# One encoder layer on one core: the opening works on 256 tokens first, with part of its statistics on ScalarE and its parameter rows spread by TensorE

## The chip, the cores and the metric

The program runs on one core of one Trainium2 chip. The metric is the device time of one execution in microseconds (us); the kernel before took 1932.78 us, the median of three runs from 1931.15 to 1933.4. Less is better. A core has five engines, each with its own queue worked in order: TensorE (PE; its weight loads are listed as PEld), VectorE (DVE), ScalarE (ACT), GpSimd (POOL) and SyncE (SP, here used to start DMA transfers; ScalarE starts some too). They wait for each other by semaphores.

## The reference

One layer of an encoder over x of 2048 tokens x 1024 features, in float32:

```python
h = layer_norm(x, in_ln_g, in_ln_b)
proj = h @ w_in[l]                       # 1024 -> 1792 features: q, k, v and u
q, k, v, u = jnp.split(proj, [Q_END, K_END, V_END], axis=-1)
... rotary on q and k; windowed attention with sinks; GLU, causal convolution of width 31, LayerNorm, silu on u
mix = jnp.concatenate([attn, conv], axis=-1) @ w_o[l]
h = layer_norm(ALPHA * h + mix, ln1_g[l], ln1_b[l])
ffn = conv_gated_mlp(h, w_up[l], ffn_conv_w[l], ffn_conv_b[l], w_down[l])
h = layer_norm(ALPHA * h + ffn, ln2_g[l], ln2_b[l])
```

The change touches the first two lines only: the first LayerNorm and the start of the projection.

## The kernel before

The phase in question (`phase_project`, tensors named a_...) takes the tokens in NB = 4 blocks of 512, each of RB = 4 rows of 128 tokens; "row (n, r)" is row r of block n. On a row this is done:

- SyncE loads it into `a_xs` (512 KB). VectorE takes two `bn_stats` of 512 columns each (`stats`), and for all four rows of the block together the aggregates, variance plus epsilon (`a_vs`), a root by ScalarE (`block_root`), a reciprocal and three small operations that refine it (`refine_rstd`), and minus mean times that (`a_nmr`).
- The row is normalised and scaled by g, then shifted by b (`scale`, `shift`, each a VectorE pass over 1024 columns). In row 3 of a block ScalarE does the normalising (`norm_last`), VectorE the product with g, GpSimd the sum with b (`shift_last`). g and b stand in `a_gb`, copied to all partitions.
- TensorE transposes the row in eight pieces of 128 x 128 (`transposes`, to `a_acc`). ScalarE rounds the result to a high part (`hi_of`), VectorE makes the low part as the rest (`lo_of`). These are the two halves of `a_hT`. Weights are split into high and low part likewise by ScalarE (`weights_hi`) and GpSimd (`weights_lo`).
- A product is three matmuls of 512 columns (high x high, high x low, low x high). `sweeps(n, first, last)` does products first to last-1 of block n: 24 of them, 8 for each of three lists of 128 output features, each list into a bank of its own (`a_mm`).

What sets the order is code written by hand. Block n-1 is swept while block n is prepared: the four transposes of block n stand between its products, after as many as `AHEAD` says. Product 0 of block n waits until `lo_of` of all four rows of block n is done. When list 1 of block n-1 is done (product 15), ScalarE loads a table and takes the gate's sigmoid (`take_gate`), which stands in its queue between `hi_of(n, 1)` and `hi_of(n, 2)`. After the opening (the four blocks) the other lists of weights follow, 4 x 8 products each, then the convolution, attention, and the feed-forward stage, all led by TensorE.

To keep TensorE at work at the start, it transposes the identity matrix into a bank that nobody reads (`keep_busy`).

## Time and profile before

| | |
|---|---|
| median of 3 runs | 1932.78 us (1931.15 to 1933.4) |
| the profiled execution's own time | 1929.07 us |
| its span (first to last instruction) | 1927.3 us |
| TensorE matmul busy | 1872.7 us, 97% |
| VectorE, ScalarE, GpSimd busy | 1533.2, 942.0, 908.5 us |

The rows of the profile come from the one profiled execution. A row names the line of the kernel, the engine, the operation and the tensors written and read. In the rows, matmuls overlap their neighbours, so a row's duration is longer than the distance to the next start. The granted clock of TensorE is 1.00 at 2.4 GHz and 0.50 at 1.2 GHz.

### The profile page before, as it was taken

The numbers are of one execution on the slowest core, as the hardware profiler recorded it, in microseconds if no ns is written. First come the engines' busy times: TensorE is split into PE (matmuls) and PEld (weight loads), VectorE is DVE, ScalarE is ACT, GpSimd is POOL, SyncE is SP. The second block draws the span as 40 slices with busy tenths as digits, with TensorE's granted clock in tenths as the row PEclk, the third lists the DMA queues.
The fourth block names the chain that finished last, engine by engine and source line by source line (L and its number), as shares of the span: only waits on it lengthen the run. The fifth ranks groups of instructions, "written<-read, shape, count | busy, mean of one in ns | idle before, by whom it ended". The sixth has DMA issues, their size and how long they took to land.

```text
span 1927.3 us, 27509 instructions
## 1 busy us (share of the span) xinstructions
PE 1872.7 (97%) x8632; PEld 1531.4 (79%) x8632; DVE 1533.2 (80%) x1945; ACT 942.0 (49%) x1469; POOL 908.5 (47%) x666
## 2 busy tenths in 40 slices
PE   8999999999999799999999799999999999999998
PEld 7788888777777588888887688888888788888886
DVE  8877993799998788878788888888888745776787
ACT  3455562777776444444445444444444433232453
POOL 2169993266675255444445544443443765530000
PEclk9999999999999899999999899999999999999999
DMA  7411123644553432323232322323234654587654
GB/s 272 174 43 44 44 82 121 204 136 146 176 189 120 148 110 95 117 93 103 103 114 77 131 104 98 118 88 109 93 120 136 197 160 134 166 253 244 186 172 143
DMA packets 200430, 258.41 MB, mean 134 GB/s; under 512 B 12208, under 2 KB 131248, under 8 KB 199856
## 3 DMA queue, kind: packets, MB, share of 16 engines
q1 hardware_dynamic: 188624, 230.37, 36.3%
q10 hardware_dynamic: 11744, 27.27, 3.8%
q8 instruction: 32, 0.52, 0.1%
q14 instruction: 30, 0.25, 0.0%
HBM read 172.98 MB, written 84.61 MB: 134 GB/s over the span
## 4 chain that ended last, share of the span: by engine, by line
PE 57%; issue 18%; DVE 11%; POOL 6%; ACT 5%; DMA 2%; SPq 1%; POOLq 0%; DVEq 0%; ACTq 0%
PE d_y L2648 21%; PE u_mm L2221 20%; PE a_mm L249 15%; POOL u_w_sum L1323 1%; ACT m_ce L1669 1%; POOL u_w_sum L1321 1%; DVE m_stat L2024 1%; DVE u_forms L1828 1%; ACT m_tps L1661 1%; POOL u_s L1341 1%; DVE m_top L2055 1%; POOL u_s L1344 1%; DVE m_den L2068 1%; POOL u_s L1338 1%; PE m_y L2270 1%
## 5 line engine op out<-in xcount | busy, mean ns | idle before, releaser
L2221 PE MATMUL u_mm<-u_forms,u_w_hi 128*128 128x512 f32 x2464 | 766.7, 393 | 26.5 <-issue 15.2
L2221 PEld LDWEIGHTS u_mm<-u_forms,u_w_hi 128*128 128x128 f32 x2464 | 466.2, 190 | 127.6 <-issue 26.4
L2221 PE MATMUL u_mm<-u_forms,u_w_lo 128*128 128x512 f32 x1232 | 482.9, 392 | 0.0
L2648 PE MATMUL d_y<-d_wd,d_a_hi 128*128 128x512 f32 x1232 | 380.9, 390 | 3.9 <-DVE d_a_lo L1032 3.8
L249 PE MATMUL a_mm<-a_hT,a_w_hi 128*128 128x512 f32 x896 | 281.2, 395 | 1.9 <-DVE a_hT L534 1.9
L2648 PEld LDWEIGHTS d_y<-d_wd,d_a_hi 128*128 128x128 f32 x1232 | 231.9, 188 | 53.0 <-DVE d_a_lo L1032 4.2
L2221 PEld LDWEIGHTS u_mm<-u_forms,u_w_lo 128*128 128x128 f32 x1232 | 233.4, 189 | 49.0
L2648 PE MATMUL d_y<-d_wd,d_a_lo 128*128 128x512 f32 x616 | 240.1, 390 | 0.0
L1859 DVE SCALAR_TENSOR_TENSOR u_y<-u_z,u_taps,u_y 128x1024 f32<-128x1024 f32 x176 | 222.6, 1287 | 15.1 <-DVE u_z L1873 3.5
L1321 POOL TENSOR_TENSOR u_w_sum<-u_w_raw 128x512 f32<-128x512 f32 x44 | 56.9, 1293 | 304.2 <-DMA u_w_raw<-w_up 304.2
L249 PEld LDWEIGHTS a_mm<-a_hT,a_w_hi 128*128 128x128 f32 x896 | 166.7, 188 | 40.3 <-DVE a_hT L534 3.5
L249 PE MATMUL a_mm<-a_hT,a_w_lo 128*128 128x512 f32 x448 | 175.2, 391 | 0.0
L1016 ACT CAST d_a_hi<-d_a_raw 128x1408 fp32r<-128x1408 f32 x56 | 77.0, 1374 | 185.8 <-PE d_y L2648 182.3
L1819 DVE TENSOR_TENSOR u_w_lo<-u_w_raw,u_w_hi 128x512 fp32r<-128x512 f32 x132 | 143.5, 1088 | 27.8 <-ACT u_w_hi L1502 27.6
L1502 ACT CAST u_w_hi<-u_w_sum 128x512 fp32r<-128x512 f32 x176 | 105.2, 620 | 116.0 <-POOL u_w_sum L1323 49.6
L1819 DVE TENSOR_TENSOR u_w_lo<-u_w_sum,u_w_hi 128x512 fp32r<-128x512 f32 x176 | 140.0, 801 | 9.9 <-ACT u_w_hi L1502 4.3
L2270 PE MATMUL m_y<-m_wo,m_mix_hi 128*128 128x512 f32 x512 | 143.4, 405 | 1.5 <-ACT m_mix_hi L1634 1.4
L472 POOL TENSOR_TENSOR a_gb<-a_gb,a_spare 128x512 f32<-128x512 f32 x112 | 130.1, 1208 | 24.3 <-ACT a_spare L391 24.3
L1032 DVE TENSOR_TENSOR d_a_lo<-d_a_raw,d_a_hi 128x1408 fp32r<-128x1408 f32 x56 | 103.5, 1848 | 44.7 <-ACT d_a_hi L1016 44.5
L2648 PEld LDWEIGHTS d_y<-d_wd,d_a_lo 128*128 128x128 f32 x616 | 116.0, 188 | 24.1
L1331 POOL TENSOR_TENSOR u_w_sum<-u_w_raw,u_w_sum 128x512 f32<-128x512 f32 x44 | 62.3, 1417 | 150.4 <-DVE u_w_lo L1819 150.4
L1552 ACT ACTIVATE u_gy<-u_y 128x1024 f32<-128x1024 f32 x44 | 45.2, 1028 | 164.9 <-DVE u_y L1859 164.9
(230 smaller groups left out, 2946.0 us busy)
## 6 DMA issues: line engine op xcount, KB each, us to landing
u_w_raw<-w_up SPq DMA_DIRECT2D x44, 1024.0 KB, 5.0
d_a_raw<-gated_scr SPq DMA_DIRECT2D x56, 704.0 KB, 5.3
gated_scr<-u_s SPq DMA_DIRECT2D x88, 256.0 KB, 2.0
d_wd_raw<-w_down SPq DMA_DIRECT2D x88, 256.0 KB, 5.1
gated_scr<-u_gy SPq DMA_DIRECT2D x44, 256.0 KB, 2.1
u_stage<-h1T_scr SPq DMA_DIRECT2D x9, 1024.0 KB, 5.5
a_xs<-x SPq DMA_DIRECT2D x16, 512.0 KB, 5.6
m_h_in<-h_scr SPq DMA_DIRECT2D x16, 512.0 KB, 4.0
```

The lines of the kernel that those rows point to most:

```text
L249: last = nc.tensor.matmul(mm[bank][:], w[:, k, :], hT[n][:, part, k, :], start=(k == 0 and w is hi and part == HI_PART), stop=(k == KT - 1 ...
L472: nc.gpsimd.tensor_tensor(p, p, prod[:, i % 2, 0:size], ALU.add).then_inc(part_ok, 1)
L1016: nc.scalar.copy(a_hi[:, u % 2, :, :], a_raw[:, u % 2, :, :]).then_inc(ahi_ok, 1)
L1032: nc.vector.tensor_tensor(a_lo[:, u % 2, :, :], a_raw[:, u % 2, :, :], a_hi[:, u % 2, :, :].bitcast(F32), ALU.subtract).then_inc(alo_ok, 1)
L1321: nc.gpsimd.tensor_tensor(w_sum[:, 0, :, :], a21, raw_of(Q4), ALU.add).then_inc(sum_ok, 1)
L1331: nc.gpsimd.tensor_tensor(w_sum[:, 0, :, :], raw_of(Q2), w_sum[:, 1, :, :], ALU.subtract).then_inc(sum_ok, 1)
L1502: nc.scalar.copy(w_hi[:, s, :, :], left_of(s)).then_inc(whi_ok, 1)
L1819: nc.vector.tensor_tensor(w_lo[:, s, :, :], left_of(s), w_hi[:, s, :, :].bitcast(F32), ALU.subtract).then_inc(wlo_ok, 1)
L1859: v = nc.vector.scalar_tensor_tensor(out=y[:, m, :], in0=z[:, m, k:k + SPAN], scalar=tap(st, m, k), in1=y[:, m, :], op0=ALU.mult, op1=ALU.add)
L2221: last = nc.tensor.matmul(mm[BANK[s]][:], w[:, s, k, :], forms[:, POS[s], part, k, :], start=(s in FRESH and k == 0 and w is w_hi and part ...
L2270: m = nc.tensor.matmul(ym[:, at], a[:, c.slot, k, :], wo_part(part, k)[:, at], start=opens, stop=closes)
L2648: m = nc.tensor.matmul(dy[u % BANKS][:], a[:, u % 2, k, :], wd[:, ph % 2, k, part, :], start=(k == 0 and a is a_hi and part == HI_PART), s ...
```

## The change

For block 0 the work is done in two pairs of rows. Rows 0 and 1 get their own variance, root and refined reciprocal (`FIRST_PAIR`), and are scaled and shifted at once; rows 2 and 3 follow. Sweep 0 is done twice, each time on 256 of its 512 columns: first for rows 0 and 1 (`FIRST_ROWS`), then for rows 2 and 3 (`LAST_ROWS`). The second of these stands where the whole sweep of block 0 stood, between the transposes of block 1, at new places of `AHEAD`. The statistics of two rows of each block are taken by ScalarE (`row_moments`: the mean as the accumulated sum of a pass, a small scaling of it, the variance as the accumulated sum of squares of a second pass): rows 2 and 3 in block 0, rows 0 and 1 in blocks 1 to 3. g and b are loaded as one row each into one partition, spread by four matmuls with a row of ones (K = 1, 512 columns, float32), and copied from the banks to `a_gb` by ScalarE (`spread`). Rows 0 and 1 of x are loaded as two halves; the transfers of positions move from ScalarE's queue to SyncE's, those of the convolution's taps and biases behind the weights and the first reload. In block 0 VectorE shifts row 3 (`shift_normed`), not GpSimd.

```diff
+        GB_BANKS = (1, 2, 3, 0)
+        FIRST_PAIR, SECOND_PAIR, WHOLE = slice(0, 2), slice(2, 4), slice(0, RB)
+
+        def on_act(n, r):
+
+            return r >= 2 if n == 0 else r < 2
+
+        def stat_at(n, r):
+
+            return 3 * (2 * n + r % 2)
+
+        def product(hi, lo, n, k, bank, cols=slice(0, BLK)):
...
-                last = nc.tensor.matmul(mm[bank][:], w[:, k, :], hT[n][:, part, k, :],
+                last = nc.tensor.matmul(mm[bank][:, cols], w[:, k, :], hT[n][:, part, k, cols],
...
         def _(sp):
-            sp.dma_start(ident[:], con[:, CON_ID:CON_ID + P]).then_inc(con_ld, 16)
-            for r in range(RB):
+            for r in range(2):
+                sp.dma_start(xs[:, r, 0:BLK], x[bass.ts(r, P), 0:BLK]).then_inc(x_ld[r], 16)
+                sp.dma_start(xs[:, r, BLK:D], x[bass.ts(r, P), BLK:D]).then_inc(x_half_ld[r], 16)
+            for r in range(2, RB):
                 sp.dma_start(xs[:, r, :], x[bass.ts(r, P), :]).then_inc(x_ld[r], 16)
-            sp.dma_start(g_bc, row_to_all(ln_g)).then_inc(par_ld, 16)
-            sp.dma_start(b_bc, row_to_all(ln_b)).then_inc(par_ld, 16)
-            sp.dma_start(taps[:], par[:, PAR_TAPS:PAR_TAPS + CT * TAPS].rearrange("p (c t) -> p c t", c=CT)).then_inc(par_ld, 16)
-            sp.dma_start(cbias[:], par[:, PAR_CB:PAR_CB + CT]).then_inc(par_ld, 16)
+
...
+            reload(0, 0)
+            sp.dma_start(taps[:], par[:, PAR_TAPS:PAR_TAPS + CT * TAPS].rearrange("p (c t) -> p c t", c=CT)).then_inc(par_ld, 16)
+            sp.dma_start(cbias[:], par[:, PAR_CB:PAR_CB + CT]).then_inc(par_ld, 16)
+            reload(0, 1)
+            store(0, 0)
+            store(0, 1)
+            reload(0, 3)
+            reload(0, 2)
+            store(0, 2)
+            store(0, 3)
+            for f in range(ROT // 2):
+                sp.dma_start(pos[f * NT:(f + 1) * NT, :], positions.rearrange("o (t q) -> (o t) q", t=NT)).then_inc(pos_ld, 16)
+            sp.dma_start(freq[:], con[:, CON_FREQ:CON_FREQ + 4]).then_inc(pos_ld, 16)
+            for n in range(1, NB - 1):
...
+            def spread(c):
+
+                dst = gb[:, c * BLK:(c + 1) * BLK]
+                act.wait_ge(gb_ps, c + 1)
+                nc.scalar.copy(dst, mm[GB_BANKS[c]][:]).then_inc(gb_ok, 1)
+
+            def row_moments(n, r):
+
+                at = stat_at(n, r)
+                act.wait_ge(x_ld[r], 16 * (n + 1))
+                if n == 1:
+                    act.wait_ge(x_half_ld[r], 16)
+                if at:
+                    act.wait_ge(act_stat, at)
+                nc.scalar.activation(unread[:], xs[:, r, :], ACT.Identity, scale=1 / D, accum_out=mv[:, r, 0:1]).then_inc(act_stat, 1)
+                act.wait_ge(act_stat, at + 1)
+                nc.scalar.activation(part_mean[:, r:r + 1], mv[:, r, 0:1], ACT.Copy, scale=1 / 32).then_inc(act_stat, 1)
+                act.wait_ge(act_stat, at + 2)
+                nc.scalar.activation(unread[:], xs[:, r, :], ACT.Square, bias=part_mean[:, r:r + 1], scale=-1 / 32,
+                                     accum_out=mv[:, r, 1:2]).then_inc(act_stat, 1)
+
+            def block_root(n, of=WHOLE):
+                act.wait_ge(veps_ok, n + 1 if of == FIRST_PAIR else n + 2)
+                nc.scalar.activation(root[:, of], veps[:, of], ACT.Sqrt).then_inc(root_ok, 1)
...
-            for f in range(ROT // 2):
-                act.dma_start(pos[f * NT:(f + 1) * NT, :], positions.rearrange("o (t q) -> (o t) q", t=NT)).then_inc(pos_ld, 16)
-            act.dma_start(freq[:], con[:, CON_FREQ:CON_FREQ + 4]).then_inc(pos_ld, 16)
-            block_root(0)
-            norm_last(0)
+            act.dma_start(gb_row[0:1, 0:D], ln_g.rearrange("(o d) -> o d", o=1)).then_inc(gb_ld, 16)
+            act.dma_start(gb_row[0:1, D:2 * D], ln_b.rearrange("(o d) -> o d", o=1)).then_inc(gb_ld, 16)
+            act.dma_start(ident[:], con[:, CON_ID:CON_ID + P]).then_inc(con_ld, 16)
+            spread(0)
+            spread(1)
+            spread(2)
+            block_root(0, FIRST_PAIR)
+            spread(3)
+            row_moments(0, 2)
+            row_moments(0, 3)
             hi_of(0, 0)
+            block_root(0, SECOND_PAIR)
             weights_hi(0)
             hi_of(0, 1)
+            norm_last(0)
             weights_hi(1)
+            weights_hi(2)
+            row_moments(1, 0)
             hi_of(0, 2)
+            row_moments(1, 1)
             hi_of(0, 3)
-            weights_hi(2)
             for n in range(1, NB):
                 e = OPEN * (n - 1)
                 block_root(n)
@@ -353,7 +412,11 @@
                 hi_of(n, 0)
                 hi_of(n, 1)
                 take_gate(e + 1, n - 1, 2)
+                if n < NB - 1:
+                    row_moments(n + 1, 0)
                 hi_of(n, 2)
+                if n < NB - 1:
+                    row_moments(n + 1, 1)
                 hi_of(n, 3)
                 take_q(e + 2, n - 1, 3)
                 store_q(e + 2, n - 1)
...
+            nc.gpsimd.memset(ones_row[0:1, :], 1.0).then_inc(half_pi_ok, 1)
...
-            pool.wait_ge(par_ld, 64)
-            shift_last(0)
             for i in range(OPEN):
                 weights_lo(i)
+            pool.wait_ge(par_ld, 32)
+            pool.wait_ge(gb_ok, 4)
...
+            def block_variance(n, of=WHOLE):
+                ours = [r for r in range(RB)[of] if not on_act(n, r)]
+                if ours:
+                    chain.wait()
+                for r in ours:
+                    chain.inc(nc.vector.bn_aggr(mv[:, r, :], stat[:, r, :, :].rearrange("p a s -> p (a s)")))
+                if ours:
+                    chain.wait()
+                if n or not ours:
+                    dve.wait_ge(act_stat, 6 * (n + 1))
+                nc.vector.tensor_scalar(veps[:, of], mv[:, of, 1], EPS, None, ALU.add).then_inc(veps_ok, 1)
+
+            def block_rstd(n, of=WHOLE):
+                at = n + 1 if of == FIRST_PAIR else n + 2
+                dve.wait_ge(root_ok, at)
+                chain.inc(nc.vector.reciprocal(inv[:, of], root[:, of]))
+                dve.wait_ge(veps_ok, at)
+                refine_rstd(nc, chain, rstd[:, of], veps[:, of], inv[:, of], tmp[:, of])
+                for r in range(RB)[of]:
+                    refined[n, r] = chain.n
+                if of == FIRST_PAIR:
+                    return
                 chain.wait()
-                for r in range(RB):
-                    chain.inc(nc.vector.bn_aggr(mv[:, r, :], stat[:, r, :, :].rearrange("p a s -> p (a s)")))
...
+            stats(0, 0)
+            stats(0, 1)
+            block_variance(0, FIRST_PAIR)
+            block_rstd(0, FIRST_PAIR)
+            dve.wait_ge(gb_ok, 4)
+            scale(0, 0)
+            shift(0, 0)
+            scale(0, 1)
+            shift(0, 1)
+            block_variance(0, SECOND_PAIR)
+            lo_of(0, 0)
+            block_rstd(0, SECOND_PAIR)
+            lo_of(0, 1)
+            scale(0, 2)
+            shift(0, 2)
+            scale(0, 3)
+            shift_normed(0, 3)
+            stats(1, 3)
             lo_of(0, 2)
+            stats(1, 2)
             lo_of(0, 3)
-            stats(1, 1)
             for n in range(1, NB):
-                stats(n, 2)
-                stats(n, 3)
-                block_stats(n)
+                block_variance(n)
+                block_rstd(n)
                 rows(n)
-                if n < NB - 1:
-                    stats(n + 1, 0)
                 lo_of(n, 2)
                 if n < NB - 1:
-                    stats(n + 1, 1)
+                    stats(n + 1, 2)
                 lo_of(n, 3)
+                if n < NB - 1:
+                    stats(n + 1, 3)
+            opening = chain.n
+            dve.wait_ge(par_ld, 32)
 
             seq = Count(ang_seq, dve)
...
-            AHEAD = {1: (14, 17, 19, 21), 2: (12, 15, 18, 21), 3: (12, 15, 18, 21)}
-
-            def keep_busy(count):
+            AHEAD = {1: (9, 16, 20, 23), 2: (12, 15, 18, 21), 3: (12, 15, 18, 21)}
+
+            def keep_busy(dst, count):
 
                 for _ in range(count):
-                    nc.tensor.transpose(mm[0][:, 0:P], ident[:], ident[:])
-
+                    nc.tensor.transpose(dst, ident[:], ident[:])
+
+            pe.wait_ge(half_pi_ok, 1)
+            pe.wait_ge(gb_ld, 32)
+            for c, bank in enumerate(GB_BANKS):
+                nc.tensor.matmul(mm[bank][:], ones_row[0:1, :], gb_row[0:1, c * BLK:(c + 1) * BLK], start=True,
+                                 stop=True).then_inc(gb_ps, 1)
             pe.wait_ge(con_ld, 16)
-            with pe.Fori(0, 9) as _:
-                keep_busy(8)
-            for r, count in enumerate((8, 16, 0, 16)):
-                transposes(0, r)
-                keep_busy(count)
+            keep_busy(tp[1][:, KT - 1, :], 24)
+            transposes(0, 0)
+            pe.wait_ge(gb_ok, 4)
+            keep_busy(mm[0][:, 0:P], 10)
+            transposes(0, 1)
+            keep_busy(mm[0][:, 0:P], 16)
+            FIRST_ROWS, LAST_ROWS = (0, 2), (2, RB)
+            sweeps(0, 0, 8, FIRST_ROWS)
+            transposes(0, 2)
+            sweeps(0, 8, 14, FIRST_ROWS)
+            transposes(0, 3)
+            sweeps(0, 14, ALL, FIRST_ROWS)
             for n in range(1, NB):
-                done = 0
+                done, of = 0, LAST_ROWS if n == 1 else (0, RB)
                 for r in range(RB):
-                    sweeps(n - 1, done, AHEAD[n][r])
+                    sweeps(n - 1, done, AHEAD[n][r], of)
                     transposes(n, r)
                     done = AHEAD[n][r]
-                sweeps(n - 1, done, ALL)
+                sweeps(n - 1, done, ALL, of)
             sweeps(NB - 1, 0, ALL)
```

TensorE's queue, where the first products of block 0 begin: before (the names: `a_acc` gets the transposed row 3, `a_mm<-a_ident` is filler, L249 the products)

```order
L636 MATMUL a_acc<-a_ident,a_h_rows 128x128 [waits a_lo,a_h_last]
L636 MATMUL a_acc<-a_ident,a_h_rows 128x128 x7
L660 MATMUL a_mm<-a_ident 128x128 x16
L249 MATMUL a_mm<-a_hT,a_w_hi 128x512 [waits a_wlo,a_lo]
L249 MATMUL a_mm<-a_hT,a_w_hi 128x512
L249 MATMUL a_mm<-a_hT,a_w_lo 128x512
```

and the same place now (`a_acc` gets row 1, L266 are the products):

```order
L730 MATMUL a_acc<-a_ident,a_h_rows 128x128 [waits a_h]
L730 MATMUL a_acc<-a_ident,a_h_rows 128x128 x7
L754 MATMUL a_mm<-a_ident 128x128 x16
L266 MATMUL a_mm<-a_hT,a_w_hi 128x256 [waits a_wlo,a_lo]
L266 MATMUL a_mm<-a_hT,a_w_hi 128x256
L266 MATMUL a_mm<-a_hT,a_w_lo 128x256
```

The products now stand behind the transposes of row 1, not of row 3, and have 256 columns instead of 512; those of block 0 are twice as many (144 matmuls for 72).

ScalarE's queue in block 1, from the high parts of rows 0 and 1 to the copy of list 2: before

```order
L312 CAST a_hT<-a_acc 128x8x128 [waits a_tp] x2
L321 ACT_TABLE_LOAD [waits a_glu]
L321 ACTIVATE a_sig<-a_mm 128x512 [waits a_mm]
L312 CAST a_hT<-a_acc 128x8x128 [waits a_tp] x2
L330 COPY a_q_out<-a_mm 128x512 [waits a_q_st0,a_mm]
```

and now (L341 to L345 are `row_moments` of rows (2, 0) and (2, 1)):

```order
L362 CAST a_hT<-a_acc 128x8x128 [waits a_tp] x2
L371 ACT_TABLE_LOAD [waits a_glu]
L371 ACTIVATE a_sig<-a_mm 128x512 [waits a_mm]
L341 ACTIVATE a_unread,a_mv<-a_xs 128x1024 [waits a_act_stat,a_x_ld0]
L343 ACTIVATE a_part_mean<-a_mv 128x1 [waits a_act_stat]
L345 ACTIVATE a_unread,a_mv<-a_xs,a_part_mean 128x1024 [waits a_act_stat]
L362 CAST a_hT<-a_acc 128x8x128 [waits a_tp]
L341 ACTIVATE a_unread,a_mv<-a_xs 128x1024 [waits a_act_stat,a_x_ld1]
L343 ACTIVATE a_part_mean<-a_mv 128x1 [waits a_act_stat]
L345 ACTIVATE a_unread,a_mv<-a_xs,a_part_mean 128x1024 [waits a_act_stat]
L362 CAST a_hT<-a_acc 128x8x128 [waits a_tp]
L380 COPY a_q_out<-a_mm 128x512 [waits a_q_st0,a_mm]
```

Six operations have come in ahead of the last two high parts of the block: three before that of row 2, three between it and that of row 3. The queue in block 2 reads the same; in block 3 it is as before.

## Rows read from the trace of the kernel before

**Rows 1.** The page's busy times (share of the span).

```profile
PE 1872.7 (97%) x8632; PEld 1531.4 (79%) x8632; DVE 1533.2 (80%) x1945; ACT 942.0 (49%) x1469; POOL 908.5 (47%) x666
```

**Rows 2.** Busy by stretch: us, then each engine, PEclk, DMA share, GB/s.

```profile
0.00:60.00 60.00, 50.56 (x295) 44.30 (x296) 50.53 (x81) 21.67 (x25) 13.28 (x12) 0.97 0.69 240
...
100.00:200.00 100.00, 100.00 (x436) 81.46 (x435) 78.80 (x66) 56.31 (x85) 79.76 (x67) 1.00 0.12 42
```

**Rows 3.** Order of time on TensorE, 0 to 92 us (start, duration).

```profile
2.85 10.38 PE L660 MATMUL a_mm<-a_ident 128*128 128x128 f32 x72 [2.85 <-DMA a_ident<-con]
18.18 1.97 PE L636 MATMUL a_acc<-a_ident,a_h_rows 128*128 128x128 f32 x8 [4.95 <-DVE a_h_rows L529]
...
22.35 1.91 PE L660 MATMUL a_mm<-a_ident 128*128 128x128 f32 x16
...
28.90 0.73 PE L249 MATMUL a_mm<-a_hT,a_w_hi 128*128 128x512 f32 x2 [0.62 <-DVE a_hT L534]
...
50.18 0.50 PE L249 MATMUL a_mm<-a_hT,a_w_hi 128*128 128x512 f32 x1 [0.78 <-DVE a_hT L534]
...
70.87 0.50 PE L249 MATMUL a_mm<-a_hT,a_w_hi 128*128 128x512 f32 x1 [0.26 <-DVE a_hT L534]
...
91.58 0.73 PE L249 MATMUL a_mm<-a_hT,a_w_hi 128*128 128x512 f32 x2 [0.27 <-DVE a_hT L534]
```

**Rows 4.** Order of time on VectorE and GpSimd, 5 to 36 us.

```profile
5.07 2.59 DVE L496 BATCH_NORM_STATS2 a_stat<-a_xs 128x6 f32<-128x512 f32 x4 [5.07 <-DMA a_xs<-x]
...
14.45 2.48 DVE L521 SCALAR_TENSOR_TENSOR a_h_rows<-a_xs,a_mv,a_gb 128x1024 f32<-128x1024 f32 x2 [1.24 <-DMA a_cbias<-par]
...
22.77 2.35 DVE L534 TENSOR_TENSOR a_hT<-a_acc,a_hT 128x1024 fp32r<-128x1024 f32 x2
...
25.34 4.74 POOL L435 TENSOR_TENSOR a_w_lo<-a_w_raw,a_w_hi 128x1024 fp32r<-128x1024 f32 x2
...
34.30 2.47 DVE L521 SCALAR_TENSOR_TENSOR a_h_rows<-a_xs,a_mv,a_gb 128x1024 f32<-128x1024 f32 x2
```

**Rows 5.** Landing of a_pos, then of a_ident, after issue (views by tile).

```profile
DMA to landing us min/median/max: 2.0/5.0/6.1
...
DMA to landing us min/median/max: 2.0/2.0/2.0
```

**Rows 6.** Order of time on TensorE: plain float32 products of 256 columns.

```profile
405.83 1.08 PE L2327 MATMUL m_pv<-m_probT,m_vw 128*64 128x256 f32 x8
```

**Rows 7.** Order of time on ScalarE where two accumulating passes stand.

```profile
1807.94 1.02 ACT L2460 ACTIVATE d_unused<-d_total 128x1024 f32<-128x1024 f32 x1
1808.89 0.19 ACT L2460 ACTIVATION_READ_ACCUMULATOR d_unused<-d_total 128x1 f32 x1
1809.37 1.12 ACT L2467 ACTIVATE d_unused<-d_total,d_minus_mean 128x1024 f32<-128x1024 f32 x1 [0.29 <-DVE d_minus_mean L2555]
...
1810.52 1.13 ACT L1028 CAST d_wd<-d_wd_raw 128x512 fp32r<-128x512 f32 x2
```

**Rows 8.** Order of time on ScalarE, blocks 1 and 2.

```profile
42.72 1.02 ACT L312 CAST a_hT<-a_acc 128x1024 fp32r<-128x1024 f32 x1 [1.95 <-PE a_acc L636]
43.76 1.28 ACT L321 ACT_TABLE_LOAD   x1
45.05 0.60 ACT L321 ACTIVATE a_sig<-a_mm 128x512 f32<-128x512 f32 x1
45.55 1.01 ACT L312 CAST a_hT<-a_acc 128x1024 fp32r<-128x1024 f32 x1
...
63.65 1.28 ACT L321 ACT_TABLE_LOAD   x1
```

**Rows 9.** Busy by stretch around idle times of TensorE (columns as in rows 2).

```profile
18.20:21.30 3.10, 3.10 (x15) 3.10 (x16) 3.10 (x3) 1.11 (x2) 0.00 (x0) 0.50 0.88 255
653.30:656.20 2.90, 2.86 (x7) 2.31 (x8) 2.90 (x6) 1.30 (x2) 0.00 (x0) 0.51 0.55 143
633.30:639.00 5.70, 5.46 (x12) 3.80 (x12) 5.56 (x7) 3.04 (x4) 0.00 (x0) 0.50 0.22 65
```

54 lines of the change are left out of this document (22 added, 32 removed).

## The prediction, made before the changed kernel ran

> **What bounds the kernel now.** I read the page first, to see the busy shares: TensorE is busy 1872.7 us of 1927.3 [rows 1]. Then busy times by stretch: TensorE is full from 100 to 200 us, but of the first 60 us it is busy 50.6 [rows 2], and much of that is filler. Then TensorE in order of time: the first real product starts at 28.90 us, and product 0 of blocks 1, 2 and 3 starts at 50.18, 70.87 and 91.58 [rows 3]. Ahead of each of these it waits for `lo_of` of row 3 (0.78, 0.26 and 0.27 us). After 91.58 TensorE leads the phase, so I take what the change does to that start as what it does to the whole time: 1 us there is 1 us at the end. The question is not when the first product starts, but when product 0 of block 3 does.
>
> From 28.90 to 91.58 there are three periods of 20.7 us (21.3 the first), in which TensorE has about 20.2 us of work: 72 matmuls at 100/436 = 0.229 us [rows 2], so 16.5, and four times eight transposes at 0.11 (16 fillers in 1.91 [rows 3]), so 3.7 with their seams. VectorE is nearly as full, ScalarE is not. So three engines are to be followed in the order of their queues. I did that for the changed queues: each operation starts when its engine is free and its semaphores have come (0.05 us after the signal), with durations from rows.
>
> **The change, part by part.**
>
> *Parameters and the first pair.* g and b now come as two small transfers on ScalarE's queue, started at about 0.9 and 1.4 us. The trace has no transfer of one row; nearest are the identity (landed 2.0 us after issue) and those of the positions, 2.0 to 6.1, median 5.0 [rows 5]. So both rows are there between 3.2 and 6.5 us; I take 4.7. The four spreading matmuls are plain float32 and 512 wide. The nearest row has 256 columns: eight in 1.08 us, two side by side, so at most 0.27 us a pair [rows 6]; without the last one's tail about 0.23, so 0.45 for 512 columns at full clock. TensorE has just begun, and before, its first 72 transposes took 0.144 each against 0.11 later [rows 3], part of them slower still; so I take half the clock, 0.9 us each: done at about 8.4. The first root stands behind three of ScalarE's copies: 8.1. VectorE's own statistics of rows 0 and 1 are done before that, by 7.7 at the latest (four halves from 5.07, 2.59 us [rows 4]). So `scale(0, 0)` starts at 9.2 instead of 14.45 [rows 4]: 5.2 us earlier.
>
> A rule of the Trainium skill speaks against this step: "FP8 and Floating Point Precision", section "TensorE Precision Notes", says that true float32 takes four passes through the array. The row of 256 columns shows about two (0.23 us a pair for 256 columns, where a column of the rounded products costs 0.229/512). By the rule each spreading matmul would cost twice what I take, the third would end 2.7 us later, and the sum would be 2.7 us higher (in rival (b)).
>
> *First products.* Scales and shifts of rows 0 and 1 take VectorE to 14.3 (1.2 each [rows 4] and small waits of one for the next). ScalarE meanwhile takes the statistics of rows (0, 2) and (0, 3), and can only then round row 0. What one row costs: first pass 1807.94 to 1809.08 with its accumulator read, 1.14; a small scaling, 0.2; second pass with read 1.15 to the next start; with hand-overs 2.55 us [rows 7]. So `hi_of(0, 0)` runs at 14.1, the second root 15.0, the weights' high part 15.2 to 16.2, and GpSimd's low part, 2.4 (two in 4.74 [rows 4]), sets the first product: 18.7 us instead of 28.90, 10.2 earlier.
>
> *Block 0 done twice at half width.* 144 matmuls of 256 columns. No row has this width of rounded float32. From below: half of 0.229 is 0.115, and a load with a 128-wide matmul takes 0.11. From above, if load and columns added up: 0.115 + 0.11 = 0.22. In the 512-wide stream the load lies beside the previous matmul (0.229 with a load each), so I take 0.12: 17.3 us for 16.5, 0.8 us more, and not on the path, since TensorE waits in the end (below). At 0.22 it would add 15.
>
> *VectorE to block 1.* From 9.2 on it has eight passes of scale and shift for block 0 (9.5 us with the shift that GpSimd did), four low parts (1.15 each, two in 2.35 [rows 4]: 4.6), statistics of two rows instead of four (2.4), and two rounds of small steps (3.1), and waits 1.6 for ScalarE and for its own results: 21.2 us. `scale(1, 0)` at 30.4 instead of 34.30 [rows 4]. Of the 10.2 us, 3.9 are left. `shift(1, 0)` is done at 34.1; TensorE has finished nine half products of the last rows at 32.5 and waits 1.6. Transposes of row (1, 0), seven products of 3 x 0.12, transposes of row (1, 1), `hi_of(1, 1)`: ScalarE is through with it at 39.6. Before, that was 43.76, where the table load starts [rows 8].
>
> *ScalarE's chain in block 1.* What follows there, up to product 0 of block 1, is serial: table 1.29, gate 0.50, (1, 2) 0.91, (1, 3) 1.0, low part 1.2, hand-overs. Two row statistics now stand in it, 5.1 us. Sum: 1.29 + 0.50 + 2.55 + 0.91 + 2.55 + 1.0 + 1.2 + 0.1 = 10.1 us, so product 0 of block 1 at 49.7. Before it was 6.4 (50.18 - 43.76, part of it TensorE's own pace). So of the lead 0.5 us is left. TensorE, done at 43.2, is idle 6.5 us; the half-width surplus and a later place in `AHEAD` are hidden in this. What is queued behind the statistics is exactly what TensorE waits for; the statistics themselves wait for nobody (the reload of row (2, 0), issued at 31.7, lands well before 41).
>
> *Block 2.* From product 0 to the table load 13.5 us as before (63.65 - 50.18 [rows 3, 8]), then 10.1 instead of 7.2 (70.87 - 63.65): 2.8 us later. What VectorE saves (two rows' statistics, 2.4 us) lies beside it. *Block 3* has no statistics to take: 20.7 as before. So product 0 of block 3 is 2.8 - 0.5 = 2.3 us later.
>
> *Clock.* After 4.95 us without work [rows 3] TensorE ran at half clock for the next 3.1 us; behind two later idle times 2.9 and 5.7 us were at 0.51 and 0.50 [rows 9]. An idle time of 6.5 us should bring the same: 3 to 5.7 us at half clock, so 1.5 to 2.9 lost, early in block 1; I take 2.0. It is not made up, since block 2's chain starts from a product.
>
> *At nothing:* SyncE's nine transfers of positions and frequencies (started from 23.4 on, behind the last store of block 0; SyncE's next is a reload at 31.7), taps and biases, x in halves, GpSimd without `shift_last(0)` (it waits for weights). The 1 MB of spread-out parameters that goes from the queue brings weights earlier, which nothing waits for.
>
> Sum: 2.3 + 2.0 = +4.3 us. The profiled execution took 1929.07 us, so it would be 1933.4; the median of the runs is 3.7 above it, and I give the time against that: 1932.78 + 4.3 = 1937.1 us.
>
> **The rivals.** A change of 0.2% (3.9 us) is about what a measurement of this kernel can tell from none.
>
> (a) As above, 1937.1, own range 1934.5 to 1940: 0.50. For it: the durations are all read, and the serial chain is short.
>
> (b) The first pair starts later, and each us of that moves everything up to `hi_of(1, 1)` and so product 0 of block 1. Either the spreading matmuls take twice as long (1.8 us each): +2.7, 1939.8, chance 0.07, against it [rows 6]; this is the page's rule. Or g and b land at 6.5, like the slowest of the positions [rows 5]: +1.8, 1938.9, chance 0.08.
>
> (c) Loads do not hide under 256 columns (0.22 us each): TensorE becomes the bound of block 1, seven products before row (1, 1) take 4.6 instead of 2.5, all of sweep 0 takes 14 more, against the 6.5 idle: about 1944. Chance 0.07.
>
> (d) Not slower: a row's statistics on ScalarE cost 2.0 us instead of 2.55, because the reads of the accumulator lie beside the next pass. Then each chain is 1.1 shorter, block 0's start too; the third start comes out even, and without a fall of the clock the time is 1932.5. It decides at 2.0 us a row: above, slower, below, not. Against it: the distances between the passes [rows 7]. Chance 0.19.
>
> (e) The gain at the start carries: ScalarE's two rows are through before TensorE has done its last product, so that block 1 starts at 46 and nothing idles. Then -4 to -5, 1928. For it: TensorE's first product is 10 us earlier. Against it: ten serial microseconds from 39.6. Chance 0.09.
>
> **How the numbers follow.** Of (a) a little over half (0.27) lies above 1936.6; with (b) and (c) slower is 0.49. The rest of (a) and (d) are the same: 0.41. Faster, from (e) and a little of (d): 0.10. The range leaves out (c) and (e): 1931 to 1942.5.
>
> **What would show it.** `scale(0, 0)` near 9.2 and the first 256-wide product near 18.7; 256-wide matmuls 0.12 apart; in ScalarE's order of time the two passes between gate and `hi_of(1, 2)`, 2.5 us a row; TensorE idle about 6 us ahead of product 0 of block 1, released by `lo_of`, and 0.50 granted after it; product 0 of block 1 at 49.7, of block 2 at 75, of block 3 at 96. I am wrong if that idle time is under 3 us or if blocks 1 and 2 start earlier than 50 and 71.

## The result, and the profile of the changed kernel

The changed kernel takes 1946.12 us (median of 6 runs, 1943.67 to 1949.06); the kernel before, beside it, 1931.3 us (6 runs, 1928.78 to 1933.4). The ratio is 1.008 (95% interval 1.0069 to 1.0091): slower, by about 15 us. The prediction said slower by 4.3 us, 1937.1, with a range up to 1942.5: the direction is right, the time lies outside the range, and 4.3 us were forecast of about 15.

The page's busy times [rows 1] hardly move; ScalarE has 22 us more, VectorE 13 less:

```profile
PE 1877.1 (97%) x8650; PEld 1533.7 (79%) x8650; DVE 1520.4 (78%) x1927; ACT 964.0 (50%) x1514; POOL 902.5 (46%) x666
```

Busy by stretch, columns as in [rows 2]. TensorE has 41.9 us in the first 60 (50.6 before), and two stretches at 0.50; from 100 to 200 us it is as full as before:

```profile
0.00:60.00 60.00, 41.90 (x269) 35.69 (x270) 44.32 (x57) 36.44 (x56) 12.04 (x12) 0.98 0.59 210
...
58.80:64.30 5.50, 5.50 (x13) 4.35 (x14) 4.95 (x13) 2.33 (x3) 0.00 (x0) 0.50 0.17 63
...
84.90:88.20 3.30, 3.29 (x8) 2.61 (x9) 2.75 (x11) 1.37 (x3) 0.00 (x0) 0.50 0.21 79
100.00:200.00 100.00, 99.73 (x443) 81.27 (x442) 69.38 (x68) 53.34 (x78) 66.32 (x54) 1.00 0.12 43
```

TensorE in order of time, answering to [rows 3]. The first product is 4.9 us earlier than before (28.90), product 0 of block 1 8.6 us later (50.18), that of block 2 14.1 later (70.87), that of block 3 15.6 later (91.58), which is the whole loss:

```profile
4.46 7.16 PE L759 MATMUL a_mm<-a_gb_row,a_ones_row 1*128 1x512 f32 x8 [4.46 <-DMA a_gb_row<-in_ln_b]
11.55 5.24 PE L754 MATMUL a_acc<-a_ident 128*128 128x128 f32 x24
...
23.98 0.50 PE L266 MATMUL a_mm<-a_hT,a_w_hi 128*128 128x256 f32 x2 [2.60 <-DVE a_hT L615]
...
58.78 1.22 PE L266 MATMUL a_mm<-a_hT,a_w_hi 128*128 128x512 f32 x2 [6.34 <-DVE a_hT L615]
...
84.92 1.22 PE L266 MATMUL a_mm<-a_hT,a_w_hi 128*128 128x512 f32 x2 [3.14 <-DVE a_hT L615]
...
107.16 0.73 PE L266 MATMUL a_mm<-a_hT,a_w_hi 128*128 128x512 f32 x2 [0.27 <-DVE a_hT L615]
```

The first row has eight records for four matmuls in the code. The value in brackets is the time in which the engine was idle, with what released it. VectorE in order of time (to compare with [rows 4]); L598 is `scale`, L605 `shift`, L594 the product with g of row 3, L611 its shift, L117 a step of the refinement on 2 columns:

```profile
12.28 1.28 DVE L598 SCALAR_TENSOR_TENSOR a_h_rows<-a_xs,a_mv,a_gb 128x1024 f32<-128x1024 f32 x1 [0.78 <-ACT a_gb L331]
...
20.16 2.05 DVE L117 TENSOR_TENSOR a_vs<-a_vs 128x2 f32<-128x2 f32 x1
...
25.23 3.34 DVE L605 SCALAR_TENSOR_TENSOR a_h_rows<-a_h_rows,a_vs,a_gb 128x1024 f32<-128x1024 f32 x1
28.50 3.40 DVE L594 TENSOR_TENSOR a_h_rows<-a_h_rows,a_gb 128x1024 f32<-128x1024 f32 x1
31.93 1.22 DVE L611 TENSOR_TENSOR a_h_rows<-a_h_rows,a_gb 128x1024 f32<-128x1024 f32 x1
...
39.41 2.47 DVE L598 SCALAR_TENSOR_TENSOR a_h_rows<-a_xs,a_mv,a_gb 128x1024 f32<-128x1024 f32 x2
```

GpSimd in order of time over the same stretch:

```profile
19.84 2.35 POOL L499 TENSOR_TENSOR a_w_lo<-a_w_raw,a_w_hi 128x1024 fp32r<-128x1024 f32 x1 [18.80 <-ACT a_w_hi L325]
25.09 2.40 POOL L499 TENSOR_TENSOR a_w_lo<-a_w_raw,a_w_hi 128x1024 fp32r<-128x1024 f32 x1 [2.91 <-ACT a_w_hi L325]
27.44 3.37 POOL L499 TENSOR_TENSOR a_w_lo<-a_q_out,a_w_hi 128x1024 fp32r<-128x1024 f32 x1
```

Lay the two beside each other: a step of 0.16 us takes 2.05 and ends with GpSimd's first pass (20.16 + 2.05 = 22.21, 19.84 + 2.35 = 22.19); `shift(0, 2)` takes 3.34 where 1.28 is normal and ends 1.08 us behind the end of GpSimd's second; GpSimd's third, begun during that shift, takes 3.37 instead of 2.4; `scale(0, 3)`, begun during the third, 3.40 instead of 1.22. `scale(1, 0)` starts at 39.41 instead of 34.30. In the kernel before, GpSimd's passes lay beside VectorE's statistics and low parts, and all had their usual length (VectorE, then GpSimd, rows that [rows 4] leave out):

```profile
28.76 3.65 DVE L496 BATCH_NORM_STATS2 a_stat<-a_xs 128x6 f32<-128x512 f32 x6
```

```profile
23.00 2.38 POOL L440 TENSOR_TENSOR a_h_rows<-a_h_rows,a_gb 128x1024 f32<-128x1024 f32 x1 [22.09 <-DVE a_h_rows L517]
...
30.01 2.43 POOL L435 TENSOR_TENSOR a_w_lo<-a_q_out,a_w_hi 128x1024 fp32r<-128x1024 f32 x1
```

ScalarE of the changed kernel in order of time, the chain of block 1 (to compare with [rows 7, 8]):

```profile
48.69 1.28 ACT L371 ACT_TABLE_LOAD   x1
49.98 0.60 ACT L371 ACTIVATE a_sig<-a_mm 128x512 f32<-128x512 f32 x1
50.48 1.05 ACT L341 ACTIVATE a_unread<-a_xs 128x1024 f32<-128x1024 f32 x1
51.43 0.19 ACT L341 ACTIVATION_READ_ACCUMULATOR a_unread<-a_xs 128x1 f32 x1
...
53.03 0.99 ACT L362 CAST a_hT<-a_acc 128x1024 fp32r<-128x1024 f32 x1
...
56.48 0.99 ACT L362 CAST a_hT<-a_acc 128x1024 fp32r<-128x1024 f32 x1
```

### The profile page after: what moved, and what is told of

It is laid out like the page before. It is cut to its first block, busy times and chain, and to the rows that moved or that the text cites. A ratio compares the mean times of both kernels' runs of the same rounds, so it can differ in the third digit from the quotient of the medians.

```text
span 1944.9 us, 27577 instructions
## 1 busy us (share of the span) xinstructions
PE 1877.1 (97%) x8650; PEld 1533.7 (79%) x8650; DVE 1520.4 (78%) x1927; ACT 964.0 (50%) x1514; POOL 902.5 (46%) x666
## 4 chain that ended last, share of the span: by engine, by line
PE 57%; issue 18%; DVE 12%; POOL 6%; ACT 5%; DMA 1%; SPq 0%; POOLq 0%; DVEq 0%; ACTq 0%
PE d_y L2754 21%; PE u_mm L2327 20%; PE a_mm L266 14%; POOL u_w_sum L1429 1%; ACT m_ce L1775 1%; POOL u_w_sum L1427 1%; DVE m_stat L2130 1%; DVE u_forms L1934 1%; ACT m_tps L1767 1%; POOL u_s L1447 1%; POOL u_s L1450 1%; DVE m_top L2161 1%; DVE m_den L2174 1%; POOL u_s L1444 1%; PE m_y L2376 1%
## 5 line engine op out<-in xcount | busy, mean ns | idle before, releaser
L266 PE MATMUL a_mm<-a_hT,a_w_hi 128*128 128x512 f32 (+1 forms) x944 | 287.1, 387 | 12.3 <-DVE a_hT L615 12.3
L266 PEld LDWEIGHTS a_mm<-a_hT,a_w_hi 128*128 128x128 f32 x944 | 174.9, 190 | 49.7 <-DVE a_hT L615 13.8
L266 PE MATMUL a_mm<-a_hT,a_w_lo 128*128 128x512 f32 (+1 forms) x472 | 180.8, 383 | 0.0
L1925 DVE TENSOR_TENSOR u_w_lo<-u_w_raw,u_w_hi 128x512 fp32r<-128x512 f32 x132 | 135.9, 1031 | 29.6 <-ACT u_w_hi L1608 29.6
```

The costliest lines, as they stand in the source:

```text
L266: last = nc.tensor.matmul(mm[bank][:, cols], w[:, k, :], hT[n][:, part, k, cols], start=(k == 0 and w is hi and part == HI_PART), stop=(k ...
L1925: nc.vector.tensor_tensor(w_lo[:, s, :, :], left_of(s), w_hi[:, s, :, :].bitcast(F32), ALU.subtract).then_inc(wlo_ok, 1)
```

## The experiments

Twelve kernels ran, each beside the kernel before on its chip. For each, from its profiled execution, the start of `scale(1, 0)` and of product 0 of blocks 1 and 3, then the median time and the ratio to before with its interval:

| kernel | scale(1, 0) | block 1 | block 3 | median us | ratio |
|---|---|---|---|---|---|
| before | 34.30 | 50.18 | 91.58 | 1931.3 | 1 |
| the change | 39.41 | 58.78 | 107.16 | 1946.12 | 1.008 (1.0069 to 1.0091) |
| statistics behind row 3 | 39.19 | 54.90 | 103.05 | 1942.18 | 1.0044 (1.003 to 1.0058) |
| two low parts zero | 37.28 | 56.66 | 104.73 | 1943.63 | 1.005 (1.0036 to 1.0064) |
| filler in the idle time | 39.14 | 58.51 | 102.79 | 1942.95 | 1.005 (1.0033 to 1.0067) |
| g, b by DMA | 38.20 | 57.59 | 106.91 | 1947.11 | 1.0079 (1.0053 to 1.0106) |
| low parts by VectorE | 37.19 | 56.58 | 102.41 | 1944.5 | 1.0067 (1.0047 to 1.0087) |
| statistics by VectorE | 39.47 | 55.17 | 96.61 | 1940.45 | 1.0046 (1.003 to 1.0061) |
| statistics in gaps | 39.86 | 55.56 | 99.84 | 1941.16 | 1.0046 (1.0029 to 1.0063) |
| four together | 37.98 | 53.67 | 99.09 | 1938.95 | 1.0041 (1.0026 to 1.0056) |
| warm-up matmuls | 39.23 | 60.15 | 108.89 | 1952.62 | 1.0097 (1.0082 to 1.0113) |
| scales early | 39.47 | 58.84 | 107.28 | 1945.84 | 1.0064 (1.0048 to 1.0079) |
| all causes put right | 32.48 | 48.18 | 89.59 | 1932.5 | 0.9998 (0.9989 to 1.0007) |
| and gate behind | 32.26 | 47.68 | 89.09 | 1932.37 | 0.9999 (0.999 to 1.0008) |

The starts are those of one execution each, the medians those of 4 to 11. The medians of the kernel before, beside them, went from 1931.3 to 1932.39, so two rows' medians that differ by under 1 us are not told apart. Median less block 3's start is 1838.6 to 1844 in all of them. So the start of block 3 tells the cause; the rest adds up to 5 us of its own (last section).

**Statistics behind row 3.**

```diff
                 take_gate(e + 1, n - 1, 2)
-                if n < NB - 1:
-                    row_moments(n + 1, 0)
                 hi_of(n, 2)
-                if n < NB - 1:
-                    row_moments(n + 1, 1)
                 hi_of(n, 3)
+                if n < NB - 1:
+                    row_moments(n + 1, 0)
+                    row_moments(n + 1, 1)
```

> Same work, but in blocks 1 and 2 ScalarE takes the statistics of rows 0 and 1 of the next block behind its rounding of row 3 instead of around row 2. Theory of the serial chain: the table load to product 0 of block 1 falls from 10.1 to about 5.0 us, TensorE idles about 1.2 us instead of 6.34 and its granted clock does not fall; product 0 of block 1 near 53.7 (58.78 now), of block 2 near 75, of block 3 near 96 (107.16 now), total about 11 us less than the changed kernel, near 1935. Rival, the loss comes from the first 40 us alone (late parameters, VectorE held up by GpSimd): less than 2 us changes.

TensorE in order of time, the rows with an idle time:

```profile
54.90 0.73 PE L266 MATMUL a_mm<-a_hT,a_w_hi 128*128 128x512 f32 x2 [2.67 <-DVE a_hT L614]
...
89.12 1.09 PE L729 MATMUL a_acc<-a_ident,a_xs 128*128 128x128 f32 x8 [2.55 <-DVE a_xs L604]
...
103.05 0.74 PE L266 MATMUL a_mm<-a_hT,a_w_hi 128*128 128x512 f32 x2 [0.27 <-DVE a_hT L614]
```

Block 1 comes 3.9 us earlier, not 5.1: without the statistics the chain from the table load (48.48) takes 6.4 us, as before, since other engines' work then ends last in it (ScalarE waits 0.63 us for the transposes of row 3). The granted clock still fell behind the wait (0.67 from 54.9 to 58.6). And 2.55 us come back as a new wait: in block 2 ScalarE's statistics end later, so VectorE has block 3's variance late:

```profile
82.14 0.17 DVE L573 TENSOR_SCALAR a_vs<-a_mv 128x4 f32<-128x4 f32 x1 [2.64 <-ACT a_unread L345]
84.45 0.18 DVE L578 RECIPROCAL a_vs<-a_vs 128x4 f32<-128x4 f32 x1 [2.14 <-ACT a_vs L350]
```

The rival (under 2 us) falls; the size expected, 11 us, too: it was 4.

**Two low parts zero.** The opening's lists 1 and 2 lose their low parts: GpSimd writes zeros in place of the difference.

```diff
-            for i in range(OPEN):
-                weights_lo(i)
+            weights_lo(0)
+            for i in range(1, OPEN):
+                pool.wait_ge(whi_ok, i + 1)
+                nc.gpsimd.memset(list_lo(i).bitcast(F32), 0.0).then_inc(wlo_ok, 1)
```

> Leaves out the low parts of weight lists 1 and 2 of the opening: GpSimd writes zeros there instead of a difference of two tiles. Theory that GpSimd's two-input pass keeps VectorE's two-input passes out: shift(0, 2) and scale(0, 3), 3.34 and 3.40 us now, take 1.28 and 1.22, scale(1, 0) starts about 4.3 us earlier (35.1 instead of 39.41), product 0 of block 3 as well, total about 4 us less, near 1942; the small step at 20.16 stays at 2.05 us, since the low part of list 0 is still there. Rival, VectorE's two passes are slow for a reason of their own or because GpSimd is busy at all: they stay above 2.5 us and the total stays within 1 us.

VectorE, then GpSimd, in order of time:

```profile
25.76 1.28 DVE L607 SCALAR_TENSOR_TENSOR a_h_rows<-a_h_rows,a_vs,a_gb 128x1024 f32<-128x1024 f32 x1
26.96 1.22 DVE L596 TENSOR_TENSOR a_h_rows<-a_h_rows,a_gb 128x1024 f32<-128x1024 f32 x1
...
34.44 1.23 DVE L617 TENSOR_TENSOR a_hT<-a_acc,a_hT 128x1024 fp32r<-128x1024 f32 x1 [1.04 <-ACT a_hT L362]
```

```profile
25.59 1.89 POOL L515 MEMSET a_w_lo<- 128x1024 f32 x2 [2.88 <-ACT a_w_hi L325]
```

GpSimd is busy at the same place (two memsets, 25.59 to 27.48), yet both VectorE passes have their normal length. So it is the reading GpSimd pass that holds them, not GpSimd at work. Of the 4.2 us given back only 2.1 reach `scale(1, 0)`: VectorE then waits 1.04 us for ScalarE in front of the last low part (with the change it waits nowhere there), and 0.35 ahead of another; and in this execution it was 0.5 us late already at `scale(0, 2)`.

**Low parts by VectorE**, nothing left out:

```diff
             shift(0, 2)
+            weights_lo(1)
             scale(0, 3)
             shift_normed(0, 3)
+            weights_lo(2)
...
```

> Nothing left out: the low parts of weight lists 1 and 2 of the opening are made by VectorE (behind shift(0, 2) and behind the shift of row 3) instead of GpSimd. Theory that two-input passes of the two engines exclude each other, and that the run with zeros was 2.5 us faster because of that: shift(0, 2) and scale(0, 3) at 1.28 and 1.22 us; the 2.4 us added to VectorE fall mostly into its waits of 1.0 and 1.7 us for ScalarE's rounding that the run with zeros showed; scale(1, 0) near 38 instead of 39.41, product 0 of block 3 about 1.5 us earlier than 107.16, total near 1944.5. Rival, that VectorE's own time is what counts: the added 2.4 us eat the gain, scale(1, 0) at 39.4 or later, no change.

VectorE in order of time, the same two operations:

```profile
24.98 1.28 DVE L605 SCALAR_TENSOR_TENSOR a_h_rows<-a_h_rows,a_vs,a_gb 128x1024 f32<-128x1024 f32 x1
...
27.31 1.22 DVE L594 TENSOR_TENSOR a_h_rows<-a_h_rows,a_gb 128x1024 f32<-128x1024 f32 x1
```

`scale(1, 0)` at 37.19, as early as with zeros: the 2.4 us of work stand in the waits. Block 1 comes 2.2 us earlier than with the change. Block 3 comes 4.75 earlier: 1.0 more because less of block 1 ran at the lower clock, and 1.5 because this time the granted clock did not fall behind the wait of 3.14 us ahead of block 2. The median moves by 1.6 only.

**Filler in the idle time.**

```diff
                 sweeps(n - 1, done, ALL, of)
+                keep_busy(mm[0][:, 0:P], {1: 52, 2: 24, 3: 0}[n])
```

> Adds filler transposes of the identity on TensorE where it waits, 52 before product 0 of block 1 and 24 before that of block 2; nothing else moves. Theory that the idle time brings the lower granted clock behind it: the clock stays at 1.00 after 58.8 and after 84.9, product 0 of block 2 comes 3.0 to 3.4 us earlier, that of block 3 about 1.5 more, total 4.5 to 5 us less, near 1941.5. Rival, the clock falls there for another reason or its fall is hidden by the wait for VectorE's low parts: product 0 of block 3 moves by less than 1 us.

TensorE in order of time, then busy by stretch:

```profile
52.02 5.84 PE L754 MATMUL a_mm<-a_ident 128*128 128x128 f32 x52
58.51 0.73 PE L266 MATMUL a_mm<-a_hT,a_w_hi 128*128 128x512 f32 x2 [0.66 <-DVE a_hT L615]
```

```profile
58.50:64.00 5.50, 5.49 (x24) 4.57 (x25) 4.95 (x13) 2.36 (x3) 0.00 (x0) 1.00 0.18 63
82.00:86.00 4.00, 3.92 (x17) 3.27 (x18) 3.46 (x12) 2.08 (x3) 0.00 (x0) 1.00 0.19 70
```

1.00 in both places. Block 1 starts as late as with the change (0.27 us apart); block 3 comes 4.4 us earlier. The clock's share is that: 4.1 us for two stretches at 0.50.

**g, b by DMA.**

```diff
-            act.dma_start(gb_row[0:1, 0:D], ln_g.rearrange("(o d) -> o d", o=1)).then_inc(gb_ld, 16)
-            act.dma_start(gb_row[0:1, D:2 * D], ln_b.rearrange("(o d) -> o d", o=1)).then_inc(gb_ld, 16)
...
+            act.dma_start(g_bc, row_to_all(ln_g)).then_inc(gb_ld, 16)
+            act.dma_start(b_bc, row_to_all(ln_b)).then_inc(gb_ld, 16)
```

> Undoes the spreading alone: g and b come by two transfers of 512 KB to all partitions on ScalarE's queue, behind the identity; no spreading matmul, no copy of its result; 56 filler transposes instead of 24. Theory that four passes of float32 at half clock cost the start 3 us: scale(0, 0) starts between 8.5 and 10.5 instead of 12.28, as early as the parameters land beside the rows of x, and scale(1, 0) and the total come 2 to 3 us earlier, near 1943.5. Rival, the transfers take as long as before (landed after 12) or the start is set elsewhere (weights, statistics on ScalarE): scale(1, 0) moves by less than 1 us and so does the total.

The filler ahead of row 0 is 56 transposes instead of 24. `scale(0, 0)` stands at 11.73, only 0.55 us earlier, because now row 1 of x lands late (its halves at 8.4 and 9.5 us instead of 6.3 and 7.3), and VectorE waits for it:

```profile
8.39 0.69 DVE L558 BATCH_NORM_STATS2 a_stat<-a_xs 128x6 f32<-128x512 f32 x1 [2.73 <-DMA a_xs<-x]
...
11.73 1.28 DVE L594 SCALAR_TENSOR_TENSOR a_h_rows<-a_xs,a_mv,a_gb 128x1024 f32<-128x1024 f32 x1
```

ScalarE, rid of four copies, ends its statistics 1.3 us earlier (16.26 instead of 17.56; it can't begin them sooner, since the root of the first pair and row 2 of x, landed at 8.7 with the change, both come at 10.75), and the first product, `scale(1, 0)` and block 1 come 1.2 us earlier. Block 3 keeps 0.25 of it, because more of block 2 ran at the lower clock, and the total does not move. So spreading by matmuls is no worse than the megabyte on the way beside x.

**Warm-up matmuls.**

```diff
+            for _ in range(8):
+                nc.tensor.matmul(tp[0][:, 0, :], ones_row[0:1, :], ones_row[0:1, :], start=True, stop=True)
             pe.wait_ge(gb_ld, 32)
```

> Eight more matmuls of the row of ones ahead of the four spreading matmuls (TensorE starts at about 1 us instead of 4.46 and has been at work for 3 us when g and b are there); nothing else moves. The spreading matmuls now take 1.70 us each with 0.50 granted, that is four cycles a column. If their price is four passes and the clock only doubles it: should the clock be granted within them, the records stand 0.43 us apart instead of 0.85, and scale(0, 0) comes up to 3 us earlier; should it not, they stay at 0.85 and nothing moves (total 1946 within 1.5 us), and the lower clock at the start is then no matter of 4 us of earlier work. Rival, a float32 matmul 512 wide costs 1.70 us at either clock: records at 0.85 with 1.00 granted.

```profile
1.00 3.78 PE L758 MATMUL a_acc<-a_ones_row 1*128 1x128 f32 x16 [1.00 <-POOL a_half_pi L494]
4.58 7.03 PE L761 MATMUL a_mm<-a_gb_row,a_ones_row 1*128 1x512 f32 x8
```

Eight matmuls of 128 columns give 16 records, 0.213 us apart behind the first, four matmuls of 512 columns again 8, 0.853 apart. The transposes right behind stand 0.213 us apart, later ones 0.109, so this is the lower level, although the view shows 1.00 there: this trace has no record of the clock before 16.2 us. Both kinds of matmul take 4 cycles a column at 1.2 GHz (2 x 0.213 x 1200 / 128 = 4.0; 2 x 0.853 x 1200 / 512 = 4.0). The other level was not reached here; the row of [rows 6], at 1.00 granted, has records 0.216 us apart for 256 columns, which is about 4 cycles a column again (2 x 0.216 x 2400 / 256 = 4.05). So the price in passes is the same at both levels, though no run shows the spreading matmuls themselves at the upper one.

The early work did not bring the full clock sooner. TensorE is at work from 1.0 us on here and from 4.5 with the change, and its transposes stand 0.213 us apart until 16.2 and 16.5; with g and b by DMA, where it has nothing but transposes to do from 4.4 on, they do so until 7.6 only. What in the spreading matmuls makes the difference (one row of the array, plain float32) is not shown.

The total is 6.5 us worse (5.4 when each kernel is set against the one before beside it). Block 1 starts 1.4 us later: behind an idle time of 1.8 us that the changed kernel has too, TensorE ran at 0.51 from 43.4 to 46.8, in the changed kernel at 1.00. Block 3 starts 1.7 later. The rest stands behind it (last section).

**Scales early.**

```diff
-            dve.wait_ge(gb_ok, 4)
+            dve.wait_ge(gb_ok, 2)
             scale(0, 0)
-            shift(0, 0)
             scale(0, 1)
+            dve.wait_ge(gb_ok, 4)
+            shift(0, 0)
             shift(0, 1)
...
```

The first root stands ahead of ScalarE's third copy.

> Same work: VectorE takes scale(0, 0) and scale(0, 1) as soon as g is spread (two copies of four) and both shifts behind them; the first root stands ahead of ScalarE's third copy. Theory that the late parameters (scale(0, 0) at 12.28 where 9.2 was forecast) cost the start of block 1 the same 3 us: scale(0, 0) near 9.7, shift(0, 1) done near 14.7 instead of 17.5, product 0 of block 1 about 2.5 us earlier and the total near 1943.5. Rival: VectorE next waits for the statistics of rows 2 and 3, which ScalarE has only at 17.4 whatever the first pair does, so that the 3 us go into that wait: the small step behind them stays near 17.6, product 0 of block 1 and the total move by less than 1 us.

```profile
12.50 2.48 DVE L605 SCALAR_TENSOR_TENSOR a_h_rows<-a_h_rows,a_vs,a_gb 128x1024 f32<-128x1024 f32 x2
17.62 0.17 DVE L574 TENSOR_SCALAR a_vs<-a_mv 128x2 f32<-128x2 f32 x1 [2.65 <-ACT a_unread L345]
```

The rival holds: both shifts are done at 14.98 instead of 17.55, and VectorE then waits 2.65 us for ScalarE's statistics of rows 2 and 3, which end at 17.6 in either kernel. `scale(1, 0)` is at 39.47. What the late spreading costs goes by ScalarE's queue, not by VectorE's: the fourth copy stands ahead of those statistics. The run without the copies agrees: statistics 1.3 us earlier, `scale(1, 0)` 1.2.

**Statistics by VectorE** (blocks 2 and 3).

```diff
-            return r >= 2 if n == 0 else r < 2
+            return n < 2 and (r >= 2 if n == 0 else r < 2)
...
```

> Undoes one part: the statistics of rows 0 and 1 of blocks 2 and 3 go back to VectorE, in the places of the kernel before; those of blocks 0 and 1 stay as they are. Theory of the serial chain, corrected by the run with the statistics behind row 3: table load to product 0 of block 1 takes 6.4 us as before, product 0 of block 1 near 54.9, that of block 2 20.7 to 22.5 later (about 76.5, with some loss to the clock behind an idle time of 3 us), that of block 3 20.7 after that, 97 to 98: about 9.5 us less than the changed kernel, near 1936.5. What is left to before, 5 us, is then the first 40 us. Rival, VectorE cannot carry four rows of statistics beside the rest in this order: product 0 of block 3 comes after 101.

Block 1 at 55.17, block 3 at 96.61, in periods of 20.7 us: near what was expected, and 5.0 us behind before. The total is 4 us above the 1936.5 expected; see the last section.

**Statistics in gaps.**

```diff
                 hi_of(n, 0)
+                if n == 2:
+                    row_mean(n + 1, 0)
                 hi_of(n, 1)
...
                 hi_of(n, 2)
+                if n == 2:
+                    row_variance(n + 1, 0)
                 hi_of(n, 3)
```

> Same work: ScalarE keeps the statistics, in block 1 behind its rounding of row 3, in block 2 the first pass of row 0 between the roundings of rows 0 and 1, its second between those of rows 2 and 3 (ScalarE waits 1.95 us in each of these places) and row 1 behind row 3. Theory that only what lies inside the chain or delays the next root costs: product 0 of block 1 at 54.9, of block 2 at 78.0, and of block 3 not 25 but 22.5 us later, near 100.5; about 6.5 us less than the changed kernel, near 1939.5. Rival, any ScalarE statistics in block 2 hold up the next block whatever their place: 103 as with both behind row 3, 1942.

Block 3 at 99.84 where 100.5 was expected: the same ScalarE work costs 7.3 us less than in the chain. It is not free here either: against the run in which VectorE takes these statistics (96.61), ScalarE's cost 10.6 us in the chain, 6.4 behind row 3 and 3.2 in the gaps, the clock's falls included.

**Four together**: gaps, low parts by VectorE, scales early, 14 filler transposes.

> Four things together, nothing left out: statistics in ScalarE's gaps, low parts of lists 1 and 2 by VectorE, scales of rows 0 and 1 as soon as g is spread and both shifts behind them (with the first root ahead of the third copy), and 14 filler transposes before product 0 of block 1. Theory that the causes are separate and add up: 6.5 + 1.5 + 2.5 + 1.5, total near 1934, still above the kernel before. Rival, a common limit behind them (VectorE's or ScalarE's sum of work up to block 1) holds the start of block 1 after 53, total above 1937.

Block 3 at 99.09, total 1938.95: the rival's side. The causes do not add: `scale(1, 0)` is only 1.4 us earlier, since ScalarE's statistics of block 0 still end at 17.5, and with ScalarE's statistics behind row 3 of block 1, row (2, 0) came 2.2 us late and the clock fell behind that (0.53 from 65.3 to 68.9).

**All causes put right.** Besides scales early and statistics by VectorE: VectorE takes the statistics of rows 2 and 3 of block 0 too, the weights' high parts stand ahead of `hi_of(0, 0)`, the filler is moved, and GpSimd's three passes wait until VectorE is in operations with one input from SBUF:

```diff
+            stats(0, 2)
+            stats(0, 3)
             block_variance(0, SECOND_PAIR)
-            lo_of(0, 0)
             block_rstd(0, SECOND_PAIR)
+            lo_of(0, 0)
             lo_of(0, 1)
...
+            pool.wait_ge(h_ok, 2)
             weights_lo(0)
+            pool.wait_ge(nmr_ok, 1)
             weights_lo(1)
+            pool.wait_ge(h_last, 1)
             weights_lo(2)
```

> Nothing left out; the changed kernel with each cause that the runs named put right. VectorE takes the statistics of rows 2 and 3 of block 0 itself (in the 2.8 us in which it waited for ScalarE's) and all of blocks 2 and 3; ScalarE keeps rows 0 and 1 of block 1, outside the chain; scales of the first pair as soon as g is spread; GpSimd's three low parts wait until VectorE is in passes with one input from SBUF (statistics and low parts); filler moved. By the durations read so far: shift(0, 1) done 14.7, first product 21.1 instead of 23.98, shift and scale at 1.28 and 1.22 throughout, scale(1, 0) near 32.5 instead of 39.41, product 0 of block 1 near 48.5, of block 3 near 89.9 (91.58 before): total near 1930, 1.5 us under the kernel before. Rival, the opening on half widths has a cost of its own that these causes do not explain (transposes and products in TensorE's order, or the clock): product 0 of block 3 after 93, total above 1934.

VectorE, then GpSimd, in order of time:

```profile
14.63 2.46 DVE L560 BATCH_NORM_STATS2 a_stat<-a_xs 128x6 f32<-128x512 f32 x4
...
18.82 2.35 DVE L613 TENSOR_TENSOR a_hT<-a_acc,a_hT 128x1024 fp32r<-128x1024 f32 x2
...
32.48 2.48 DVE L596 SCALAR_TENSOR_TENSOR a_h_rows<-a_xs,a_mv,a_gb 128x1024 f32<-128x1024 f32 x2
```

```profile
14.79 2.38 POOL L493 TENSOR_TENSOR a_w_lo<-a_w_raw,a_w_hi 128x1024 fp32r<-128x1024 f32 x1 [13.76 <-DVE a_h_rows L603]
18.98 2.38 POOL L493 TENSOR_TENSOR a_w_lo<-a_w_raw,a_w_hi 128x1024 fp32r<-128x1024 f32 x1 [1.81 <-DVE a_nmr L585]
26.31 2.38 POOL L493 TENSOR_TENSOR a_w_lo<-a_q_out,a_w_hi 128x1024 fp32r<-128x1024 f32 x1 [4.95 <-DVE a_h_rows L609]
```

The same three GpSimd passes lie beside VectorE's statistics (one input) and low parts (one input from SBUF, one from the bank), and neither engine is slowed. First product 21.22, `scale(1, 0)` 32.48, block 1 48.18, block 3 89.59 (expected 21.1, 32.5, 48.5, 89.9). Block 3 is 17.6 us earlier than with the change, which had lost 15.6. The total is 1932.5, ratio 0.9998: no difference from before that the runs can tell. The interval goes from 2.1 us less to 1.4 more, so the 2 us by which block 3 starts earlier lie just inside it.

**And gate behind.** `take_gate` moves behind `hi_of(n, 3)`.

> The kernel with every cause put right, and one thing more that its own trace points to: ScalarE's table load and gate (1.29 + 0.50 us) stand behind its roundings of rows 2 and 3 in each block instead of ahead of them. Theory that they are the longest item left in the serial chain to product 0: that of block 1 comes 1.8 us earlier (46.4 instead of 48.18), TensorE idles under 1 us there instead of 2.66, the later periods fall from 20.7 by at most 0.3 us each, product 0 of block 3 near 87.3; the total is 2 us less than with the gate ahead, near 1930, 0.1% under the kernel before. Rival: ScalarE is not the last in that chain (TensorE's own products and transposes, or VectorE's low parts, end at the same time): product 0 of block 1 moves by less than 0.6 us and the total stays at that of the kernel before.

The rival holds: block 1 comes 0.5 us earlier, block 3 0.5, and the total doesn't move. ScalarE now waits 1.51 us for TensorE's transposes ahead of row 2 (its row in order of time):

```profile
43.03 1.02 ACT L362 CAST a_hT<-a_acc 128x1024 fp32r<-128x1024 f32 x1 [1.51 <-PE a_acc L734]
```

No version here is faster than the kernel before by more than the measurement can tell.

## Why the prediction was right in direction and too small

The direction had been given a chance of 0.49, and luck has a part in it: the prediction's own terms, ScalarE's chain and the clock, hold and make 4.3 of the 15.6 us by which block 3 starts later; the largest of the others, the meeting of GpSimd's and VectorE's passes, it did not have at all. The sum should have ended with product 0 of block 3 2.3 us late and 2 us for the clock, so near 96; it was 107.16. Step by step:

- *Parameters and the first pair* failed in its size: `scale(0, 0)` at 12.28, not 9.2. TensorE's wait for g and b ended at 4.46 (4.7 taken). The spreading matmuls took 1.70 us each (two records of 0.853), not 0.9: the row of 256 columns [rows 6] was misread. Its eight records are four matmuls of the code, so a pair side by side took twice the 0.23 us. The half clock was taken rightly. The rule that the prediction weighed and put aside, the Trainium skill's "FP8 and Floating Point Precision", section "TensorE Precision Notes" (four passes for true float32), agrees with the trace: the records give 4.0 cycles a column.
- *First products*: 23.98, not 18.7. ScalarE's fourth copy came at 11.66 (8.9 by the forecast; row 2 of x was there at 8.7), its two statistics behind it, `hi_of(0, 0)` at 17.70 instead of 14.1, the weights' high and GpSimd's low part after that. And the small step that took 2.05 us held up `lo_of(0, 1)`, which released the product. So the spreading's 3 us are on the path, by ScalarE's queue; the run with scales early shows that VectorE's late start beside it is not. That `hi_of(0, 0)` stands behind two row statistics was in the forecast; it is their late start that it had wrong.
- *Block 0 at half width* was right: matmuls of 256 columns stand mostly 0.12 us apart, 0.113 to 0.125 (0.12 taken; rival (c) had 0.22).
- *VectorE to block 1* is the step that failed most: 27.1 us from `scale(0, 0)` to `scale(1, 0)`, where 21.2 were summed. The terms are right one by one; missing is what GpSimd's low parts do to them, 1.9 + 2.1 + 2.2 us = 6.1 with the unrounded rows on three VectorE operations. In the kernel before, GpSimd's passes lay from 23.0 to 32.4 beside VectorE's low parts and statistics [rows 4] and slowed nothing; the prediction moved them without asking which of VectorE's operations they now meet. The runs show it from both sides: writing instead of reading frees VectorE, VectorE doing the low parts itself does so too, and the same passes beside one-input operations slow nobody. The Trainium skill states it in "SBUF — State Buffer", section "Who interferes with whom": a VectorE instruction with two SBUF inputs contends with a GpSimd instruction that reads SBUF, not with one that only writes. The same section calls the ports that the two share an exclusive lock. The traces agree: the small step ends with GpSimd's pass to 0.02 us, GpSimd's third ends 2.24 us behind the end of the shift that it met, about its own length, and two memsets do no harm.
- *ScalarE's chain in block 1* was right to 0.1 us: 48.69 to 58.78 is 10.1, 2.55 a row; TensorE idle 6.34 (6.5 said), released by `lo_of`. So was that of the chain without them, 6.4 (behind row 3). *Block 2* was 23.6 us by the sum and 26.1 by the trace, which is the next term.
- *Clock*: one stretch at 0.50 was taken, 2.0 us; there were two, and filler in both places gave back 4.1 us of block 3's start.

Added up against 95.9 us (the step list without the clock's 2.0 is 93.9): late parameters 3.1, blocked VectorE 5.9, the chain 0.1, clock 0.6 more in block 1 and 1.5 in block 2, makes 107.1; measured 107.16. These terms are differences between the forecast's starts and the trace's, so they must add up; they do not say what each cause gives back alone. The first two overlap, since VectorE, freed of either, waits for ScalarE, which is late as well: the 3.1 us gave back nothing at `scale(1, 0)` (scales early), 4.2 of the blocked 6.1 gave 2.1 to 2.2, and only with ScalarE's statistics of block 0 moved too did `scale(1, 0)` come 6.9 us earlier.

Rival (b) had two forms. The first, spreading matmuls at twice the price, holds: `scale(0, 0)` was 3.1 us late where 2.7 were priced. It had a chance of 0.07, and its time of 1939.8 lacks the other causes. The second, g and b late, does not hold, and (c) does not; (d) fell on 2.55 us a row; (e) has its number in the kernel with all causes put right, which shows that the opening on 256 tokens can be had at no loss, but gives 2 us at block 3 and none that can be told in the total.

## What to carry to other kernels

When an engine's pass moves, list what the other engines do at its new time, GpSimd and VectorE above all: two inputs from SBUF against a reading GpSimd pass cost 2 us each time, one input costs nothing. Work handed to an engine with idle time is free only where it neither stands in a serial chain nor holds up the next block's root; the same four row statistics (two each in blocks 1 and 2) cost 10.6 us at block 3 in one place and 3.2 in another. A start 5 to 10 us earlier is worth what the slowest queue lets through: follow it to the first product of the last block of the phase before counting it. And count the records of a row against the matmuls in the code before a duration is taken from it.

## What the runs showed of the hardware that was not expected

Plain float32 matmuls show two records each (8 for 4, 16 for 8), with 2 cycles a column in each, at either level of the clock. While TensorE did such matmuls with one row, and for 3.7 to 6.1 us of transposes behind them, it stayed at the lower level, 11 to 15 us from its first work on. With transposes alone it was at the upper one after 4.9 us (the kernel before) and 3.2 us (g, b by DMA).

Which idle times bring the lower clock is not the same in each kernel. Behind 1.8 us of waiting ahead of row (1, 0) it fell in the run with warm-up matmuls and not in the changed kernel; behind 3.14 us ahead of block 2 it fell with the change and not with low parts by VectorE; behind 2.6 us ahead of the first product it fell in the run with scales early (0.50 from 23.9 to 29.9) and not in the changed kernel. The first of these falls put block 1 1.4 us later, the second block 3 1.5 us; the third cost block 1 nothing (58.84 against 58.78), since TensorE has waits to spare there. Near 380 us, after the opening, TensorE's two idle times are 0.24 and 1.46 us in the run with low parts by VectorE and 0.23 and 1.46 with the change, but the granted clock is not the same; the first, then the second kernel, TensorE by stretch at the same place of the program:

```profile
364.40:387.40 23.00, 21.19 (x104) 0.93 0.49 155
```

```profile
369.20:392.20 23.00, 21.20 (x112) 1.00 0.50 158
```

This fall cost 1.5 us. Added up over each trace, such falls are most of what differs behind block 3. From block 3's start to the end of the span it is 1835.7 us before and 1837.7 with the change, and 31 and 34 us of that (up to 1900 us) are at the lower clock; with warm-up matmuls and with statistics by VectorE it is 1842.9 and 1844.9, with 44 us at the lower clock. Over all 14 traces the time behind block 3 goes up by 0.53 us with each us at the lower clock (correlation 0.92), where half speed would cost 0.5. By this estimate the clock makes about 7 of the 9.2 us between the extremes, and in the kernel with all causes put right (34 us) about 1.7 of the 3.4 us that it takes longer behind block 3 than the kernel before. These are single executions, and what decides whether the clock falls stays open.
